# Three loads of normed rows and three result stores of a gather stage, each as 16 transfers of 8 partitions in place of one of 128

## The reference, cut to what matters

```
h2 = rms_norm(x, ffn_norm_w)
expert, gate = top 16 of each head, softmax of their scores
u = u_tab[expert]
act = gelu(einsum('td,ted->te', h2, u))
v = v_tab[expert]
x = x + einsum('te,ted->td', gate * act, v)
```

## Time and profile before

| What | Value |
|---|---|
| Median of 3 runs | 3,175.93 us |
| Lowest, highest | 3,174.69, 3,179.19 us |
| The profiled execution, its own time | 3,177.51 us |
| Span of the profiled execution, first to last instruction | 3,175.7 us |
| Mean granted TensorE clock in it | 0.950 of full speed |
| Busy: PE, DVE, ACT, POOL | 88%, 58%, 28%, 23% of the span |
| Moved by the queue of GpSimd's gathers | 536.90 MB in 73,728 packets |
| Moved by the queue of SyncE | 301.98 MB in 115,992 packets |

### The profile page before, as it was taken

One profiled execution on the slowest core, in us unless ns is written; L12 is line 12 of the kernel. 1 busy time (PEld: TensorE's weight loads), 2 busy tenths in 40 slices (PEclk: granted clock), 3 DMA queues, 4 the chain that ended last, 5 costly groups with the idle time before them and its releaser, 6 DMA issues. The chain is left out here.

```text
span 3175.7 us, 29207 instructions
## 1 busy us (share of the span) xinstructions
PE 2800.9 (88%) x10768; PEld 1850.8 (58%) x10768; DVE 1844.7 (58%) x3601; ACT 904.1 (28%) x1684; POOL 737.6 (23%) x724
## 2 busy tenths in 40 slices
PE   7999999999899989999999988877777777777877
PEld 6888587766677667889877873333333333333333
DVE  6762545343543656555635478777777777777554
ACT  3112313433355736422422332111111111111111
POOL 0000200000110513254000124333333333333331
PEclk8999999999999999999999999889889999899999
DMA  7585254521545564543623369999999999999996
GB/s 261 174 290 185 79 206 157 184 92 47 179 155 184 161 218 179 202 142 111 222 80 113 120 252 410 422 422 422 422 422 422 422 422 422 422 422 422 422 422 280
DMA packets 189863, 840.76 MB, mean 265 GB/s; under 512 B 17044, under 2 KB 19348, under 8 KB 123287
## 3 DMA queue, kind: packets, MB, share of 16 engines
q0 software_dynamic: 73728, 536.90, 40.7%
q1 hardware_dynamic: 115992, 301.98, 27.9%
HBM read 828.34 MB, written 144.71 MB: 306 GB/s over the span
## 5 line engine op out<-in xcount | busy, mean ns | idle before, releaser
L230 DVE TENSOR_TENSOR weights_low<-weights_raw,weights_high 128x2048 fp32r<-128x2048 f32 x108 | 250.5, 2319 | 420.3 <-ACT weights_high L225 410.4
L225 ACT CAST weights_high<-weights_raw 128x2048 fp32r<-128x2048 f32 x108 | 206.0, 1908 | 608.4 <-PE proj_banks L288 594.9
L288 PE MATMUL proj_banks<-h_low,weights_high 128*128 128x512 f32 x896 | 356.3, 398 | 18.9 <-PEq L161 6.2
L288 PE MATMUL proj_banks<-h_high,weights_low 128*128 128x512 f32 x896 | 351.3, 392 | 0.0
L288 PE MATMUL proj_banks<-h_high,weights_high 128*128 128x512 f32 x896 | 351.1, 392 | 0.0
L3095 ACT ACTIVATE coef<-dots 128x4 f32<-128x4 f32 x127 | 26.1, 205 | 803.4 <-DVE dots L2977 803.4
L3076 ACT ACTIVATE sig<-shape_consts,coef 128x128 f32<-128x128 f32 x512 | 163.7, 390 | 250.8 <-DVE coef L2996 247.6
L288 PEld LDWEIGHTS proj_banks<-h_low,weights_high 128*128 128x128 f32 x896 | 169.8, 189 | 57.1 <-issue 22.0
L288 PEld LDWEIGHTS proj_banks<-h_high,weights_low 128*128 128x128 f32 x896 | 169.8, 189 | 36.5 <-issue 1.9
L288 PEld LDWEIGHTS proj_banks<-h_high,weights_high 128*128 128x128 f32 x896 | 169.8, 189 | 35.8
L2887 PE MATMUL work_banks<-rows_over_split,sig 128*128 128x512 f32 x256 | 139.6, 683 | 55.9 <-ACT sig L3076 55.9
(11 more groups left out here) (515 smaller groups left out, 5673.4 us busy)
## 6 DMA issues: line engine op xcount, KB each, us to landing
joined_rows<-in_peer_u_dram SPq DMA_DIRECT2D x64, 1024.0 KB, 7.3
joined_rows<-in_peer_v_dram SPq DMA_DIRECT2D x64, 1024.0 KB, 7.3
weights_raw<-in_w_in_dram SPq DMA_DIRECT2D x36, 1024.0 KB, 5.1
weights_raw<-in_ret_w_in_dram SPq DMA_DIRECT2D x24, 1024.0 KB, 5.2
ret_gate<-in_mod_w_dram SPq DMA_DIRECT2D x20, 1024.0 KB, 12.9
weights_raw<-in_fox_w_in_dram SPq DMA_DIRECT2D x16, 1024.0 KB, 5.5
weights_raw<-in_ret_w_out_dram SPq DMA_DIRECT2D x8, 1024.0 KB, 5.1
weights_raw<-in_peer_w_q_dram SPq DMA_DIRECT2D x8, 1024.0 KB, 6.6
```

The lines of the kernel that those rows point to most:

```text
L225: nc.scalar.copy(whi[h][:, :, :], raw[h][:, :, :]).then_inc(high_ready[h], 1)
L230: nc.vector.tensor_tensor(wlo[h][:, :, :], raw[h][:, :, :], whi[h][:, :, :].bitcast(F32), ALU.subtract).then_inc(w_split[h], 1)
L288: last = nc.tensor.matmul(out_tile, lhs, rhs, start=(start and j == 0), stop=(stop and j == 2))
```

## The change

A constant STRIP = 8 is added. The loads of the rows of tiles 1, 2 and 3 are each issued as 16 transfers of 8 partitions (8 rows of 4 KB, 32 KB) in place of one transfer of 128 partitions, all raising the same semaphore. The stores of tiles 0, 1 and 2 are issued in the same way. The load of tile 0 and the store of tile 3 stay single transfers. The waits are for 256 in place of 16 where a transfer is split.

```diff
+        STRIP = 8
...
                         if t + 1 < TT:
-                            sp.dma_start(xr[:, :], h_away[:, t + 1, :]).then_inc(h_loaded[t + 1], 16)
+                            for r in range(0, P, STRIP):
+                                sp.dma_start(xr[r:r + STRIP, :], h_away[r:r + STRIP, t + 1, :]
+                                             ).then_inc(h_loaded[t + 1], 16)
                         sp.wait_ge(y_added, t + 1)
-                        sp.dma_start(out[0, t * P:(t + 1) * P, :], x[:, t, :]).then_inc(out_stored[t], 16)
-                    for t in range(TT):
-                        sp.wait_ge(out_stored[t], 16)
+                        if t + 1 < TT:
+                            for r in range(0, P, STRIP):
+                                sp.dma_start(out[0, t * P + r:t * P + r + STRIP, :], x[r:r + STRIP, t, :]
+                                             ).then_inc(out_stored[t], 16)
+                        else:
+                            sp.dma_start(out[0, t * P:(t + 1) * P, :], x[:, t, :]).then_inc(out_stored[t], 16)
+                    for t in range(TT - 1):
+                        sp.wait_ge(out_stored[t], 16 * (P // STRIP))
+                    sp.wait_ge(out_stored[TT - 1], 16)
...
-                        dve.wait_ge(h_loaded[t], 16)
+                        dve.wait_ge(h_loaded[t], 16 * (P // STRIP) if t else 16)
```

## The result

| | Kernel before | Changed kernel |
|---|---|---|
| Median of 5 runs | 3,178.3 us | 3,197.95 us |
| Lowest, highest | 3,174.69, 3,185.14 us | 3,191.96, 3,201.25 us |
| Ratio, changed to before (95% interval) | | 1.0062 (1.0052 to 1.0073) |
| Span of the profiled execution | 3,175.7 us | 3,196.2 us |

The change makes the kernel slower by 0.62%, some 20 us. I had forecast 3,169.8 us and a range up to 3,186.

A forecast was written before the change was run, and what follows sets the result against it. One late DMA engine was taken to bound the gather stage; relief of five transfers at 1.23 us, -6.2 us, with the load of tile 1, issue time and crowding near nothing, gave 3,175.93 - 6.2 = 3,169.8 us, range 3,167.5 to 3,186.

The forecast's parts named there:

- What bounds the kernel: Gather stage, from about 1,895 us: one late DMA engine ends 13.8 to 18 us after the others; VectorE waits for it.
- The cost of one transfer, 1.23 us: Gather stage: each 512 KB load or store costs the late engine 1.23 us, 6.17 us for five.
- A piece of 8 rows runs on eight engines, always the same: Split loads and stores: eight engines carry 16 rows of a transfer instead of 8, the other eight none; 1.23 us per transfer.
- If the late engine is not among the eight, it is relieved of 5 x 1.23 = 6.17 us.: Two loads, three stores in the saturated stretch: late engine outside the eight still ends last; total -6.2 us, chance 0.46.
- rival D: Gather stage: the late engine is one of the eight, carries 6.17 us more, 3,182.1 us and c on top; chance 0.22.
- Crowding, c at most 0.05 us: Split transfers: c, extra time per packet of a piece, taken near 0; each of the eight engines carries 80 such packets.
- a row whose packets were eight times smaller: 8-row load of 512 B rows at kernel start: eight packets served within a quarter microsecond, so c near 0.
- The estimate of 0.45 us: Split transfers: c if four 4 KB rows all meet on one port of about 27 GB/s; sum about +28 us.
- The load of tile 1 at nothing: Stage start: engines run nearly dry at 1,903 us, so splitting this load costs nothing; otherwise 1.23 us either way.
- SyncE's issue time at nothing: SyncE: sixteen issues take about 6 us, with 140 us to spare for loads; cost 0, uncovered 6 us each load.
- What D would show: Changed profile under D: seven landings around store 2 take 19.9 us; one engine alone at the end grows to 25 us.
- Wrong would be: any idle DMA share between 2,000 and 3,100 us: Gather stage: any idle DMA share there, or VectorE waiting for the normed rows, would show the prediction wrong.

## Why the prediction was wrong, point by point

- *What bounds the kernel.* Right: one late DMA engine sets the pace of the landings. The 7.4 us of eight instruction packets, and the -1.2 us when store 2 takes eight rows off the late engine, confirm it.
- *The cost of one transfer, 1.23 us.* Right: eight rows more cost 1.26 to 1.28, 24 more cost 3.9, eight fewer save 1.2.
- *A piece of 8 rows runs on eight engines, always the same.* Right. SyncE's queue has 116,664 packets in the changed kernel in place of 115,992: 96 x 8 - 6 x 16 = 672 completion writes more. That the engines are the same each time the stores in pieces of 8, 4 and 2 rows show.
- *"If the late engine is not among the eight, it is relieved of 5 x 1.23 = 6.17 us."* This is the step that failed first, and it turned the sign. The engine is among the eight. I had no row for the side, and gave the forecast more than twice the chance of rival D. D's mechanism held, +1.26 for each of three stores and both loads, 6.3 us in all.
- *Crowding, c at most 0.05 us.* This is the second step that failed, and the larger one: without it D would have ended near 3,182 us, inside the range. Beyond the second eight rows the two loads cost 4.3 and 5.4 us more. Spread over the late engine's sixteen packets of a load, as the prediction counted, that is 0.27 and 0.34 us each. But the count itself had the wrong place: the loaded rows took about 0.22 us in place of 0.16, so c proper was near its bound, and most of the price lay on the gathers' packets on all sixteen engines, which the sum had left alone. For the stores c was 0, as forecast. I had treated loads and stores alike and leaned on a row whose packets were eight times smaller. In the runs the crowding is less with every second partition (3.4 and 3.8 us a load) and least with every fourth (1.3 and 1.5). The Trainium skill, "SBUF — State Buffer", section "Door 1: The DMA port swizzle", puts four neighbouring partitions on one port, and by it every fourth partition of a block of 32 has a port of its own. The direction agrees, though the HBM rows move apart too, and the 1.3 to 1.5 us that stay are not explained by it. The estimate of 0.45 us that I had worked out from the Trainium skill's figure of about 27 GB/s a port, for rows that all meet, was too high for the loads, and nothing of it was seen in the stores.
- *The load of tile 1 at nothing, SyncE's issue time at nothing.* Right within the 0.7 us by which the start of the table is uncertain. The timeline of SyncE shows 5.4 us for sixteen issues, and VectorE did not wait for the normed rows.
- *What D would show.* I had written that the engine would be alone for 25 us. It is alone for 13, as before. Part of this was a slip in my own reasoning: the other seven of the eight carry the same sixteen rows as the late one and gain no lead. But the eight engines without pieces should then have ended some 12 us further ahead, a long stretch with a share near 0.5, and that is not there: the share falls from 1.02 to 0.29 and 0.06 within ten microseconds. The engines that ran dry from about 2,600 us on explain it: a lead ends where the issued gathers end. That this alone held the lead down is argued, not shown by a run.
- *"Wrong would be: any idle DMA share between 2,000 and 3,100 us."* It came, with 0.94 from 2,912 to 2,920 us. The late engine was not idle by it, since the difference in landings stays the same across it.

The sum as it should have been: 6.3 us for the eight rows on five transfers, 9.7 us for the crowding of two loads, 16.0 us; the traces gave 14.3 and 14.8.

## What to carry to other kernels

When the landings of large transfers set the pace, look for the moment when the DMA share falls to one sixteenth at the end of the stage: it shows that one engine lags, and then only that engine's work counts. How far it lags is read from it only while the other engines never run out of issued work. Splitting a transfer into pieces of 8, 4 or 2 rows put all of its bytes on fewer engines, always the same, where pieces of 16 did not (store 2: +1.3 us in pieces of 8, 0 in pieces of 16). So before doing it find out with one store in pieces of 8, 4 and 2 rows on which side the late engine lies. Loads in pieces of neighbouring rows also slowed the saturated stream beside them, at the same full DMA share and a lower rate, 360 in place of 423 GB/s.

## What the runs showed that I had not expected

- Loads into eight neighbouring partitions cost the late engine 4.3 to 5.4 us beyond their rows; stores from eight neighbouring partitions cost nothing beyond theirs. Why the direction matters is open, and so is whether the loads meet in SBUF or in HBM: the stores' rows lie 4 KB apart in HBM, those of the loads 16 KB.
- One 8 KB packet of VectorE's instructions costs its DMA engine 0.9 to 0.97 us, three times the 0.31 us (2.49 / 8) of an 8 KB row of a gather.
- Engines ran out of issued gathers in the changed kernel, with the stores alone and with more VectorE no-ops. They did not in the kernel before, nor with pieces of 16 rows, where the rate behind load 3 stays at 419 GB/s or more.
- A transfer in partition steps of 4 or 2 takes longer to issue: sixteen pieces 10.30 us on SyncE in place of 5.40, which was hidden here.

The timeline of SyncE for the loads alone and for the loads at every fourth partition:

```profile
2549.47 5.40 SPq L2910 DMA_DIRECT2D x_row<-h_away  x16
```

```profile
2548.26 10.30 SPq L2910 DMA_DIRECT2D x_row<-h_away  x16
```
